# Two decoder layers in another order: decayed attention and memory heads first, moba heads last, output halves by turn

## The reference

```
h = rms_norm(x, g_pre[l]);  u = h @ w_in[l]
(qa, ka, va, ga, qb, kb, vb, gb, rb, qm, gm) = split(u)
oa = moba(rms(qa), rms(ka), va) * silu(ga)                 # 8 heads of 64, causal, with ALiBi
log_a = log_sigmoid(rb @ w_gate_up[l] + b_gate_up[l]) / 16
ob = rms_norm(gla(qb, kb, vb, log_a)) * silu(gb)           # 4 heads, decayed linear attention
mk, mv = split(rms_norm(mem, g_mem[l]) @ w_mem_kv[l])
om = softmax(rms(qm) @ rms(mk)^T / 8) @ mv * silu(gm)      # 4 heads over 256 memory rows
x = x + concat(oa, ob, om) @ w_out[l]
```

## Time and profile before

| | |
|---|---|
| median of 3 runs | 1663.18 us (1661.44 to 1663.93) |
| the profiled execution | 1669.52 us, span 1667.6 us |
| mean granted clock of TensorE | 0.966 of full speed |
| TensorE busy | 1467.2 us, 88% |
| weight load, VectorE, ScalarE busy | 883.6 us, 638.4 us, 510.7 us |
| chain that ended last | TensorE 48%, DMA 40%, VectorE 7%, ScalarE 4% |
| expert weights | 191 transfers of 2048 KB and two halves of one |

### The profile page before, as it was taken

The page is one execution under the profiler, slowest core; times in us unless marked ns, Lnnn a source line. Parts: engine busy times, 40 slices in busy tenths (PEclk is TensorE's granted clock), DMA queues, the critical chain, the costliest instruction groups (busy, mean ns, idle before and its releaser), DMA issues.

```text
span 1667.6 us, 20664 instructions
## 1 busy us (share of the span) xinstructions
PE 1467.2 (88%) x8585; PEld 883.6 (53%) x8585; DVE 638.4 (38%) x1416; ACT 510.7 (31%) x1089; POOL 0.2 (0%) x4
## 2 busy tenths in 40 slices
PE   7997999798999999979998888888988888887886
PEld 5785878577877788844443333333333333333332
DVE  6665476455755565651221211211211211212112
ACT  5665466546564575411111011010010101010102
POOL 0000000000000000000000000000000000000000
PEclk9999799889999999979999999999999999999998
DMA  7242243233412445789999999999999999999995
GB/s 272 102 152 102 95 146 103 100 125 122 152 58 102 152 151 194 281 323 407 428 426 429 426 427 428 428 426 428 428 427 427 428 428 426 428 427 427 427 427 224
DMA packets 74452, 496.42 MB, mean 298 GB/s; under 512 B 6224, under 2 KB 10608, under 8 KB 49392
## 3 DMA queue, kind: packets, MB, share of 16 engines
q1 hardware_dynamic: 74352, 495.03, 73.0%
HBM read 493.96 MB, written 1.05 MB: 297 GB/s over the span
## 4 chain that ended last, share of the span: by engine, by line
PE 48%; DMA 40%; DVE 7%; ACT 4%; issue 1%; SPq 0%; DVEq 0%; ACTq 0%
DMA arena<-in_expert_w 39%; PE ps L1095 20%; PE ps L1438 5%; PE ps L1445 3%; DVE arena L1968 3%; PE ps L1459 3%; PE ps L1470 2%; PE ps L1092 2%; PE ps L1191 1%; PE ps L1075 1%; ACT arena L1562 1%; DVE w_lo L1968 1%; PE ps L1422 1%; ACT arena L1565 1%; PE ps L1126 1%
## 5 line engine op out<-in xcount | busy, mean ns | idle before, releaser
L1438 PE MATMUL ps<-arena 128*32 128x512 f32 x2048 | 252.2, 611 | 119.5 <-DMA arena<-in_expert_w 119.3
L1965 DVE COPY arena<-ps 128x512 f32<-128x512 f32 (+2 forms) x203 | 114.7, 588 | 531.2 <-PE ps L1438 428.0
L1565 ACT ACTIVATE arena<-ps 128x512 f32<-128x512 f32 (+6 forms) x244 | 121.6, 500 | 568.2 <-PE ps L1459 274.5
L1445 PE MATMUL ps<-arena 128*128 128x512 f32 x512 | 255.2, 621 | 0.0
L1968 DVE TENSOR_TENSOR w_lo<-arena,w_hi 128x512 fp32r<-128x512 f32 (+2 forms) x304 | 200.0, 672 | 132.5 <-ACT w_hi L1565 130.9
L1565 ACT ACTIVATE w_hi<-arena 128x512 fp32r<-128x512 f32 (+2 forms) x320 | 193.2, 620 | 101.1 <-PE ps L1095 88.2
L1438 PEld LDWEIGHTS ps<-arena 128*32 128x32 f32 x2048 | 54.2, 110 | 268.2 <-DMA arena<-in_expert_w 178.2
L1095 PE MATMUL ps<-w_hi,hT_hi 128*128 128x512 f32 (+3 forms) x448 | 175.0, 391 | 5.9 <-DVE w_lo L1968 3.6
L1470 PEld LDWEIGHTS ps<-arena 128*128 128x128 f32 x1024 | 130.4, 193 | 88.1 <-issue 84.3
L1095 PE MATMUL ps<-w_hi,hT_lo 128*128 128x512 f32 (+3 forms) x448 | 167.2, 373 | 0.0
L1095 PE MATMUL ps<-w_lo,hT_hi 128*128 128x512 f32 (+3 forms) x448 | 167.1, 373 | 0.0
(11 more groups left out here) (153 smaller groups left out, 1446.8 us busy)
## 6 DMA issues: line engine op xcount, KB each, us to landing
arena<-in_expert_w SPq DMA_DIRECT2D x191, 2048.0 KB, 31.8
arena<-in_w_in SPq DMA_DIRECT2D x23, 2048.0 KB, 7.8
arena<-in_w_out SPq DMA_DIRECT2D x6, 2048.0 KB, 7.9
arena<-in_w_in SPq DMA_DIRECT2D x3, 1536.0 KB, 6.5
arena<-in_w_mem_kv SPq DMA_DIRECT2D x2, 2048.0 KB, 9.1
arena<-in_w_branch_hgrn SPq DMA_DIRECT2D x2, 2048.0 KB, 7.8
arena<-in_w_branch_mla SPq DMA_DIRECT2D x2, 2048.0 KB, 7.7
arena<-in_mla_w_uq SPq DMA_DIRECT2D x2, 1152.0 KB, 5.5
```

The lines of the kernel that those rows point to most:

```text
L1438: o = e.matmul(B[32 * j:32 * j + 32, :], Xs[:, k, q:q + 32], Wn[:, k, :], start=i == 0, stop=i == 1)
L1445: i = e.matmul(acc[t][h][:, :], CT[ex % 2][:, t * 128:t * 128 + 128], Ys[:, h * 512:h * 512 + 512], start=ex == 0, stop=ex == NE - 1)
L1565: return e.activation(o, i, ACTF.Copy, scale=scale)
L1965: return e.tensor_copy(o, i)
```

## The change

- In both layers the decayed attention's and the memory heads' projections come first (`gb`, in layer 0 `mem0` and `mem1`, `qkv`, `qm`), then `q`, `k`, `va` and `ga` of moba. The memory heads run before the moba heads, and the order of transfers follows.
- The output projection's two halves are taken together, in four banks: planes 4 to 7 of the first, then of the second half, then planes 0 and 1 of each, then 2 and 3 of each (`BY_TURN`; weights are prepared in that order as well, kind "pair").
- In layer 0 the memory rows are turned and their statistics made beside `gb`; angles and sines are spread over `qkv` to `ga`, in place of a generator of their own.
- The transposes of q, qm and mk heads fall due one tick later.
- The forget gate's lower bound (`bounds`) moves from the start of the second block to the end of layer 1, its memory to another address, and its transfer two projections earlier, after the decayed attention of layer 1.
- SyncE issues the memory rows and `w_gate_up` ahead of the second weights, the bigger part of the constants and the positions behind them.

```diff
--- before.py
+++ after.py
@@ -40,11 +40,12 @@
...
 LEV = [(1, 32), (2, 64), (3, 128)]
-ORDER = (("q", "k", "va", "gb", "qkv", "mem0", "mem1", "qm", "ga"),
-         ("q", "k", "va", "gb", "qkv", "qm", "ga"))
+ORDER = (("gb", "mem0", "mem1", "qkv", "qm", "q", "k", "va", "ga"),
+         ("gb", "qkv", "qm", "q", "k", "va", "ga"))
 COLS = {"gb": (2560, 2944), "qkv": (2048, 2560), "qm": (2832, 3344), "ga": (1536, 2048),
...
 PLANES = (0, 1, 2, 3, 4, 5, 6, 7)
+BY_TURN = ((4, 5, 6, 7), (0, 1), (2, 3))
 NRW = 6
@@ -178,7 +179,7 @@
...
         for c0 in (0, 512):
-            out.append(("split", rows(A["w_out"][l])[:, :, c0:c0 + 512], 8, 512, None))
+            out.append(("pair", rows(A["w_out"][l])[:, :, c0:c0 + 512], 8, 512, None))
     w = rows(A["w_in_2"][0])
@@ -207,6 +208,9 @@
...
             parts += [(u, q, n, None) for q in range(k)]
+        elif kind == "pair":
+            if uses[u - 1][0] == "pair":
+                parts += [(u + h - 1, q, n, None) for ks in BY_TURN for h in range(2) for q in ks]
         elif kind == "whole":
@@ -260,6 +264,16 @@
...
 
+    def piece(lhs, k, jobs, first, final):
+        while not queue:
+            assert prepare()
+        p = queue.popleft()
+        while prepare():
+            pass
+        add("mult", p, lhs, k, jobs, first, final)
+        P.final[lhs] = p
+        tick()
+
     def mult(lhs, jobs, out, ready):
@@ -267,17 +281,10 @@
...
         for k in range(8):
-            while not queue:
-                assert prepare()
             while not ready(k):
...
                 yield
-            p = queue.popleft()
-            while prepare():
-                pass
-            add("mult", p, lhs, k, [(t, c0, n, bs[b], o) for t, c0, n, b, o in jobs], k == 0, k == 7)
-            P.final[lhs] = p
-            tick()
+            piece(lhs, k, [(t, c0, n, bs[b], o) for t, c0, n, b, o in jobs], k == 0, k == 7)
             if k % 2 == 1 and k < 7:
@@ -363,7 +370,7 @@
...
         chain((1, step("heads sum", l, what, sq, buffers=sq)), (1, step("heads root", l, what)), (1, normed),
-              (2, turned(0)), (1, turned(1)))
+              (2 if what == "k" else 3, turned(0)), (1, turned(1)))
 
@@ -422,16 +429,6 @@
...
 
-    def rotary():
-        add("angles")
-        for _ in range(4):
-            yield
-        for i in range(2):
-            add("turns", i)
-            yield
-            add("sine", i)
-            yield
-
     PAIR = [(0, 0, 512, 0, 0), (1, 0, 512, 1, 0)]
@@ -439,6 +436,10 @@
...
         def projections():
+            if l == 0:
+                for k2 in range(0, 8, 2):
+                    after(4 + k2 // 2, lambda k2=k2: turn("mem", k2, ("mT", k2)))
+                stats("mem", 8)
             for q in ORDER[l]:
@@ -463,9 +464,14 @@
...
                     yield from mult(("h", l), PAIR, bs, there)
+                    if l == 0 and q == "qm":
+                        add("sine", 0)
+                        after(2, step("turns", 1))
                     yield from heads(l, q, bs)
...
                     yield from mult(("h", l), PAIR, bs, there)
+                    if l == 0 and q == "ga":
+                        add("sine", 1)
                     add(q + " out", l, bs)
@@ -474,24 +480,23 @@
...
                     done.add(q)
-                if l == 0 and q == "q":
-                    stats("mem")
-                if l == 0 and q == "va":
-                    for k2 in range(0, 8, 2):
-                        after(2 + k2 // 2, lambda k2=k2: turn("mem", k2, ("mT", k2)))
+                if q == "mem1":
+                    chain((2, step("angles")), (2, step("turns", 0)))
+                if l == 1 and q == "ga":
+                    after(6, step("bounds"))
                 yield
...
         def softmaxes():
-            while ("k", l, 1) not in done:
-                yield
-            yield from attention(("moba", l), 8)
             while ("qm", l, 1) not in done or ("mk", l, 1) not in done:
...
             turn_out(1, 6)
+            while ("k", l, 1) not in done:
+                yield
+            yield from attention(("moba", l), 8)
 
@@ -501,7 +506,7 @@
...
         def decayed():
-            while ("vb", l) not in done or (l == 0 and "mem1" not in done):
+            while ("vb", l) not in done:
                 yield
@@ -509,16 +514,25 @@
...
                 yield
-            for half in range(2):
-                bs = []
-                yield from mult(("o", l), PAIR, bs, lambda k: ("oT", l, k // 2 * 2) in done)
-                add("residual", l, half, bs)
-                put(*bs)
-                for k2 in (4 * half, 4 * half + 2):
-                    after(3 + k2 % 4 // 2 - half, lambda k2=k2: turn(l + 1, k2, ("hT", l + 1, k2)))
+            while len(P.pool) < 6:
+                tick()
+                yield
+            bs = [[get(), get()] for _ in range(2)]
+            for h, k in [(h, k) for ks in BY_TURN for h in range(2) for k in ks]:
+                while ("oT", l, k // 2 * 2) not in done:
+                    tick()
+                    yield
+                piece(("o", l), k, [(t, 0, 512, bs[h][t], 0) for t in range(2)], k == 4, k == 3)
+                if k == 3:
+                    add("residual", l, h, bs[h])
+                    put(*bs[h])
+                    for k2 in (4 * h, 4 * h + 2):
+                        after(2 + k2 % 4 // 2 * h, lambda k2=k2: turn(l + 1, k2, ("hT", l + 1, k2)))
+                elif k % 2:
+                    yield
             stats(l + 1, 2)
 
-        run(projections(), softmaxes(), gated(), decayed(), outs(), *([rotary()] if l == 0 else []))
+        run(projections(), softmaxes(), gated(), decayed(), outs())
 
@@ -538,8 +552,6 @@
...
         yield from mult(("h", 2), PAIR, bs, there)
-        if half == 0:
-            add("bounds")
         yield from until(lambda: P.left("sq", 2))
...
@@ -1040,7 +1052,7 @@
...
         HEADS = {"mem": 4, "moba": 8, "mla": 8}
-        BEFORE = {("mem", 0): ("moba", 0), ("moba", 1): ("mem", 0), ("mem", 1): ("moba", 1)}
+        BEFORE = {("moba", 0): ("mem", 0), ("mem", 1): ("moba", 0), ("moba", 1): ("mem", 1)}
 
...
@@ -2705,15 +2717,15 @@
...
             weights(0)
-            e.dma_start(cst[:, 128:NCS], A["cst"][:, 128:NCS]).then_inc(s_cst, 16)
-            e.dma_start(posi[:, :], A["pos"]).then_inc(s_cst, 16)
-            weights(1)
             e.dma_start(memx, A["mem"].rearrange("a (t p) d -> p (a t) d", p=128)).then_inc(s_mem, 16)
...
                 e.dma_start(wgu[0:16, l * 128:l * 128 + 128], A["w_gate_up"][l]).then_inc(s_gu[l], 16)
+            weights(1)
+            e.dma_start(cst[:, 128:NCS], A["cst"][:, 128:NCS]).then_inc(s_cst, 16)
+            e.dma_start(posi[:, :], A["pos"]).then_inc(s_cst, 16)
             for u in (*range(2, NU - 2), NU - 1, NU - 2):
-                if u == 22:
-                    w.wait_ge(*at("fin", ("moba", 1), 7))
+                if u == 20:
+                    w.wait_ge(*at("ob", 1, 1))
                     e.dma_start(lb, A["hg_lower_bound_2"].partition_broadcast(128)).then_inc(s_lb, 16)
```

More of the change, by code:

```diff
@@ L892, in program @@
         v = mem(88, 2048).rearrange("p (t c) -> p t c", t=2)
-        lb = mem(96, 2048).rearrange("p (r c) -> p r c", r=2)
+        lb = mem(150, 2048).rearrange("p (r c) -> p r c", r=2)
         qnT = mem(96, 2048).rearrange("p (h s) -> p h s", h=8)
@@ L2295, in vector @@
                     for t in range(2):
-                        ts(rt[:, t * 32:t * 32 + 32], c("invf"), pf[:, t:t + 1], None, ALU.mult).then_inc(mark(dve_out), 1)
+                        ts(rt[:, t * 32:t * 32 + 32], c("invf"), pf[:, t:t + 1], None, ALU.mult).then_inc(
+                            mark(dve_out, ("angles", t)), 1)
                 elif kind == "turns":
@@ L2299, in vector @@
                     ang, nn, rr = rt[:, 0:64], rt[:, 64:128], rt[:, 128:192]
+                    w.wait_ge(*at("angles", 1))
                     if i:
                         w.wait_ge(*at("rope", 0))
-                    else:
-                        w.wait_ge(*book.newest)
                     ts(nn, ang, 1.0 / 6.283185307179586, (0.0, 0.25)[i], ALU.mult, ALU.add).then_inc(mark(dve_out), 1)
@@ L2309, in vector @@
                     w.wait_ge(*book.newest)
-                    stt(rr, nn, -6.28125, ang, ALU.mult, ALU.add).then_inc(mark(dve_out), 1)
+                    stt(rr, nn, -6.28125, ang, ALU.mult, ALU.add).then_inc(mark(dve_out, ("turns", i)), 1)
                 elif kind == "sine":
@@ L2313, in vector @@
                     nn, rr = rt[:, 64:128], rt[:, 128:192]
-                    w.wait_ge(*book.newest)
+                    w.wait_ge(*at("turns", i))
                     stt(rr, nn, -0.0019350051879882812, rr, ALU.mult, ALU.add).then_inc(mark(dve_out), 1)
```

## The result

The changed kernel takes 1648.73 us (median of 4 runs, 1646.61 to 1649.60), the kernel before 1663.56 us (1661.44 to 1664.78): a ratio of 0.991, 95% interval 0.9893 to 0.9927, or 14.8 us. The range of 1628 to 1656 holds it; the forecast of 1641.5 was 7 us too low. One run of the kernel before, made beside experiments 2 to 5, took 4099.78 us and is left out of their ratios.

What follows compares the result with a forecast made beforehand. Work ahead of the fixed expert-weight stream, bound by TensorE and its granted clock, sets the time. Gains 9.4 + 3.3 + 5.0 + 4.0 = 21.7 us take the profiled 1669.5 to 1647.8, less 6.3 to 1641.5 us for the median; range 1628 to 1656.

Steps and rivals of the forecast that it cites:

- Some 23 us at the lower level: Each layer's end before the change: 23 us of 77.4 at TensorE's lower clock, about 10 us lost.
- Layer 0, 13.4 forecast with the front: Gain of 9.4 us at layer 0's end (12.1 lost instead of 21.5) plus 4.0 at the front.
- the new loss of 3.6: Front of layer 0: ScalarE's work during mem0's eight pieces costs 3.6 us, leaving 4 of 7.6 as gain.
- The gap before the last planes: TensorE waits behind moba's last transposes, as ScalarE awaits next weights: 3.4 us in layer 0, 5.0 to 5.4 in layer 1.
- the turn: Start of the next layer: little cover behind the residuals, about 1.6 us at the first piece, up to 1.0 at the fifth.
- The 2.6 us wait stays: Decayed attention's tile 1, each layer: TensorE still waits 2.6 us for VectorE, since its neighbours are as before.
- moved for nothing: Steps said to gain nothing: decay's small product, angle and sine steps, memory's load, the lower bound's address.
- Layer 1, 3.3 forecast: Layer 1's end: 18.2 us lost instead of 21.5, with 3.1 for the bound's wait and 4.5 for clock dips.
- Block 2, 5.0 forecast: Start of block 2: 5 us come back when the forget gate's bounds leave, including a 3.71 us transpose wait.
- the slow case: Rival: VectorE or ScalarE bounds 22 moba rounds, 1.3 us more each costing 28 us: 1669; chance 0.07.
- given back at the stream: Rival: the expert stream starts at the same time whatever the layers do: 1663; chance 0.07.
- ScalarE in more places: Rival: ScalarE bounds more places, each 2 to 3 us and a dip; four cost 11 us: 1653; chance 0.22.

Runs made afterwards that it cites:

- Experiment 2: Changed kernel with the output projection's two halves one after the other again: 1650.87 us, ratio 0.9917 to the kernel before.
- experiment 3: Changed kernel with the forget gate's lower bound computed at the start of the second block again: 1648.82 us, ratio 0.9905.
- experiment 4: Changed kernel with the lower bound two pieces later in layer 1, behind the last moba head's exponentials: 1648.24 us, ratio 0.9904.
- experiment 5: Changed kernel with the next layer's first weight rounding held back behind the output's last transposes (the late rounding): 1642.73 us, ratio 0.9868.
- experiment 1: The kernel before, unchanged, profiled a second time: span 1661.9 us, against 1667.6 in the first profile.
- experiment 10: Kernel of experiment 5 with the two sines put beside the SiLU of ga (layer 0) and of gb (layer 1): 1642.56 us, ratio 0.9875.
- experiment 8: Changed kernel with the transposes of the q, qm and mk heads due after two pieces again instead of three: 1652.86 us, ratio 0.9928.
- experiment 7: Changed kernel with one more planner round before the first products of the second decayed tile: 1655.62 us, ratio 0.9942.
- experiment 6: Kernel of experiment 5 with the lower bound computed later, behind piece 154: 1642.14 us, ratio 0.9859.
- experiment 9: Kernel of experiment 5 with the lower bound moved forward in layer 1, to the sixth piece of va: 1644.66 us, ratio 0.9891.
- experiment 11: Kernel of experiment 5 with both the lower bound in va and the later sines: 1642.43 us, ratio 0.9876.
- experiment 12: Kernel of experiment 11 with the lower bound one piece later, behind the copy of the last transposed k heads: 1643.97 us, ratio 0.9865.

## Why the prediction was right in sign and 7 us too far

- *The sum, against the profile:* 21.7 forecast, 20.8 measured. **The step that failed is the last one**, "it stands 6.3 us above the median of 1663.18, so 1641.5 us for the median". It carries the same excess over to the new kernel. The excess of that one execution was low clock, most of it behind the two waits of 5.0 us (experiment 1), so the change removed it with the waits, and the sum had already counted it as gain: the profile of the changed kernel (1648.79 us) stands at its own median. "Some 23 us at the lower level" was 17 and 20 us in the second profile, by the same formula: (1 - 0.89) x 77.4 / 0.5 and (1 - 0.87) x 77.1 / 0.5. Half of the difference is 3.0 and 1.5 us, and the front has no low stretch there (clock 1.00 in 14.15 to 96 us), 1.7 us less to win. By these clocks the sum is 15.5 us instead of 21.7, and 1663.6 - 15.5 gives 1648; this is an estimate.
- *Layer 0, 13.4 forecast with the front:* 12.2, and 8.7 against the second profile. That the first is near is partly luck. The front gained about 6 us instead of 4.0 (an estimate, by the prediction's way of counting), since the new loss of 3.6 didn't come: TensorE is idle for 0.2 us in 14.06 to 60 us, against 5.85. So the rest of the layer gained about 6 us and not 9.4. The gap before the last planes was 3.4 forecast and 2.8 measured, with the mechanism as told (rounding of 88 ahead of the copy, a load issued late); the turn 1.6 and 1.5, the second wait there (up to 1.0) did not show. SiLU of ga between exponentials: 0.5 forecast, 0.4.
- *"The 2.6 us wait stays":* in layer 1; in layer 0 it is 3.9 us, as the sine behind qm and the step `turns` put 0.5 us of ScalarE and 0.8 us of VectorE ahead of it (without them 2.6, experiment 10). The prediction has these steps under "moved for nothing".
- *The front:* the 5.0 us before the heads' transposes went, but not for the third piece of cover; with two they don't come back (experiment 8). So the new order of the layer took the wait away, with the memory rows' steps that moved along; no run parts the two.
- *Layer 1, 3.3 forecast:* 3.6 (1.8 against the second profile). The bound's wait was 3.1 forecast, 2.5 measured. The gap before the last planes was forecast at 5.0 to 5.4 and is 2.4, because the two are not a sum: the load runs while TensorE stands at the bound. Without the bound in front it is 4.8 (experiment 3), near what was worked out. TensorE's idle time in the layer hardly changed (12.2 before, 11.7 after); its gain is clock. The forecast had 2.5 us more idle time and 5.8 us less lost to the clock, so that 3.3 is near 3.6 because two errors cancel.
- *Block 2, 5.0 forecast:* 3.6. Of the 3.7 us wait 1.2 stay as two smaller ones (0.9 and 0.3).
- *Rivals:* moba's rounds don't show the slow case (TensorE's longest waits of 134 to 200 us are 2.8 and 1.5 us, neither in a moba round), and nothing was given back at the stream. "ScalarE in more places" has 1653, 4 us above the measured time, and did not come true where it was expected, in the front and at the SiLU of ga.
- *Table loads:* in the changed kernel the load at the bound and what follows it read

```profile
329.37 1.28 ACT L1569 ACT_TABLE_LOAD   x1 [1.88 <-DVE arena L1980]
330.66 1.06 ACT L1574 ACTIVATE arena<-arena 128x1024 f32<-128x1024 f32 x1
331.63 0.47 ACT L1577 ACTIVATE arena<-ps 128x384 f32<-128x384 f32 x1
332.11 1.28 ACT L1569 ACT_TABLE_LOAD   x1
```

Each switch takes 1.28 us and the activation behind it follows at once; the idle time ahead of the first ended with VectorE. The Trainium skill ("ScalarE: Activation LUTs", "What ACT_TABLE_LOAD costs") has about 2.66 us with a drain; no row here shows the drain.

## What to carry to other kernels

Before a forecast goes from one profiled execution to a median, ask where the execution lost its excess. If it lies in the stretches that the change repairs, the sum counts it as gain already and it must not be subtracted once more: 1647.8 us, the forecast for the profiled execution, was right for the median too (1648.73). Waits in a row on one in-order engine behind one late transfer are not a sum; find the latest release and count from it. And before a step is moved away from a wait, look at what stands behind it on the helper engine in its new place: here a rounding that waited for memory stood ahead of a copy that TensorE needed, and putting it behind the copy at the end of both layers was worth 6 us (1642.73 us; no other version is measurably better). The lower bound made TensorE wait some 2.5 to 4 us wherever it stood, and none of its places was measurably better than another.

## What the hardware showed

- Nearly the same wait has a different price from execution to execution: after the unchanged 5.0 us waits one profile has 0.85 of the clock over each layer's end, the other 0.89 and 0.87, and most of the 5.7 us between the spans lies behind these waits.
- The length of a wait alone doesn't say whether the clock falls. In the 8 us behind layer 0's gap of 2.7 to 2.9 us the clock is 0.79 to 0.82 in three kernels (the changed one, experiments 4 and 7) and 1.00 in two (experiments 3 and 8). In the 8 us behind layer 1's wait of 2.5 us it is 0.60 in the changed kernel, 0.79 in experiments 8 and 10, and 1.00 in experiments 5 and 7.
- Behind a gap of 1.5 us at the same place in layer 0 the clock stayed at 1.00 in all six profiles with the late rounding (experiments 5, 6 and 9 to 12). Experiment 2, where a wait of 1.4 us stands just ahead of such a gap, is not among them; its clock fell there.
